# A four-layer model step on one core: zero products at the start, and new orders of work in the odd layer

## The chip, the cores and the metric

The kernel runs on one core of a Trainium2 chip. The metric is device time in microseconds, the median of the runs; the kernel before took 1620.36 us (three runs, 1618.04 to 1621.01). A core has TensorE (in the profile PE, with its weight loads as PEld), VectorE (DVE), ScalarE (ACT), GpSimd (POOL) and SyncE (SP), which run their own programs and meet at semaphores; SP issues all transfers here.

## The reference

All data are float32, x is 256 tokens by 1024. Two blocks follow each other:

- The first block has two layers. Each projects the RMS-normed x to 4096 columns, runs four retention heads and four attention heads of width 128 over the 256 tokens, gates them with silu, projects back (`w_out`) and adds; then it adds `sigmoid(rms_norm(x) @ w_ple_gate) * rms_norm(p @ w_ple)`.
- The second block has an even layer (an RWKV-7 recurrence beside a multiscale pool), an expert stage, an odd layer and a second expert stage. The odd layer is what the change touches:

```python
u = h @ w_in
q, k, v, u_s5 = jnp.split(u, ...)
q = apply_rope(rms_norm_2(q, q_norm), cos, sin)
k = apply_rope(rms_norm_2(k, k_norm), cos, sin)
o = diff_attention(q, k, v, lam)          # per head: softmax of map 0 minus lam times softmax of map 1, times v
o = rms_norm_2(o, subln, SUBLN_EPS) * (1.0 - lam_init)
o_ssm = s5_mixer(u_s5, ...)               # 32 state-space groups, gelu, then z * sigmoid(z @ w_glu)
return jnp.concatenate([o_attn, o_ssm], axis=-1) @ w_out
```

- An expert stage routes each token to 2 of 32 experts (hidden width 512) and reads the weights of all 32.

## The kernel before, in words

**Memory.** Projection weights come through a ring of six slots of 2 MB (`weight_ring`), in the order of `ring_chunks`. `g.send(sp, n)` (line 247) issues all chunks up to number n, each behind the semaphore that frees its slot; `g.chunk(pe, i)` makes TensorE wait for a chunk. The expert stages use the same slots and some areas of `arena`, `mix` and `hT` for their 2 MB pieces (`in_moe_weights`), six for a pair of experts; a loop over the pairs (line 2503 on SP, issuing through line 2490) loads a piece when the pair three before has released its place.

**The start (`first_layers`).** SP issues x of token tile 0 and x of tile 1, the resident constants (identity and small tables), the gain column, two ring chunks, and then the rest. For each tile ACT squares x in two halves with a sum (line 352) and takes a root (363); DVE inverts it and scales x into `x_normed` (368, 369). TensorE transposes the eight 128x128 squares of a tile (379) into two banks, and DVE writes them out to `hT` with the gain (391). The projections of the first chunks are 16 products of 128x512 each (808): unit 0 works on tile 0, then come the transposes of tile 1, then units 1 to 3. DVE handles tile 0 whole, its evacuation among it, before `eps` of tile 1.

**The odd layer (`odd_layer`).** Eight projections `project(j)` go to TensorE: 0 and 1 give u of the S5 groups (line 2085), 2 to 5 give q and k of the two token tiles, 6 and 7 give v of the tiles (322). SP waits for their count `s_prj` before it loads pieces of the expert stage into slots. TensorE's order is:

- projections 0 to 2, the S5 inputs (2100, 256 small products), projections 3 to 5;
- the S5 outputs in four steps a, each 32 products of K (2115) and 64 of the states (2122); ACT takes a gelu of each step (1902);
- project(6); transposes of q and k in four groups (2134), each behind the gelu of the same number, whose bank it takes, and all behind `s_qk`, DVE's rotation of q and k (1982 to 1994);
- the products of the GLU in two halves (2153), with scores(0) and scores(1) between them (2143, 2144); project(7);
- the head loop: transposes of the attention map (2182), scores(h + 2) for h = 0 and 1, product with v (2189 to 2191) once ACT has copied the map (1919). Ahead of head 2 stands the first part of the first output product (`out_part(0)`, line 2168, 8 products);
- the rest of the output products, then the router and the expert stage.

DVE runs `masked(h)` (adds the causal mask, takes the maximum; 2004 to 2010) and `attention(h)` (2016 to 2024) in the order m0, m1, a0, a1, the product of z with the sigmoid (2041), m2, m3, a2, a3. ACT runs `exps(h)` (1893) between them, the sigmoids (1912) and `copy_out(7)` (1885): exps 0 and 1, the sigmoids, copy_out(7), the copies of heads 0 and 1, exps 2 and 3, the copies of heads 2 and 3. `scores(h)` writes two banks that `masked(h - 2)` has read; the buffers `pb` and `attn` are double, by h % 2. The orders are written out by hand, and each engine follows its own.

```python
            for h in range(HT):
                if h == 2:
                    pe.wait_ge(s_z, 2)
                    pe.wait_ge(s_mk, 3)
                    out_part(0, (4, 5, 6, 7))
                pe.wait_ge(s_at, h + 1)
```

Of the kernel before, what the change touches and what calls it, by code (L numbers as in the profile page):

```python
# [13 lines left out]
P = 128  # L14
S = 256
TT = S // P
# [245 lines left out]
def bank2(ps):  # L262
    return ps[:, :].rearrange("p (a t) -> p a t", a=2)
# [156 lines left out]
def first_layers(g):  # L420
# [47 lines left out]
    s_tok = [g.sem(f"first{l}_ple_in_landed") for l in range(DEPTH)]  # L468
    s_wide = [g.sem(f"first{l}_wide_gains_landed") for l in range(DEPTH)]
    s_m, s_t, s_r, s_rc = g.sem("table_masked"), g.sem("tables_spread"), g.sem("bias_rows"), g.sem("bias_rows_copied")  # L470
    s_w, s_b = g.sem("bias_rows_written"), g.sem("bias_landed")
    norm_sems = TileNorm.sems(g, "first_norm")
    n_in = [TileNorm(g, norm_sems, 2 * l, (128, 144, 192)[l], gcol[l], (2, 3)) for l in range(DEPTH + 1)]
    n_ple = [TileNorm(g, norm_sems, 2 * l + 1, 160 + 16 * l, None, (2, 3)) for l in range(DEPTH)]
# [17 lines left out]
    with nc.Block() as block:  # L492
        @block.sync
        def _(sp):
            for tt in range(TT):
                sp.dma_start(g.x[:, tt, :], A["x"][0, tt * P:(tt + 1) * P, :]).then_inc(s_x[tt], 16)
            sp.dma_start(g.res[:, :], A["c_res"]).then_inc(s_res, 16)
            sp.dma_start(gcol[0], A["norm_g"][0]).then_inc(s_gain[0], 16)
            g.send(sp, 2)
            sp.wait_ge(s_m, 1)  # L500
            sp.dma_start(table[0:BUCKETS, :], A["rel_bias"]).then_inc(s_tab, 16)
            sp.dma_start(consts, A["c_first"]).then_inc(s_c, 16)
            sp.dma_start(ptok, A["p"][0, 0].rearrange("(a p) n -> p a n", p=P)).then_inc(s_tok[0], 16)
            for l in range(DEPTH):
                for i, name in enumerate(("q_norm_g", "k_norm_g")):
                    sp.dma_start(qkg[l][:, i:i + 1], A[name][l].rearrange("(d o) -> d o", o=1)).then_inc(s_qkg[l], 16)
            g.send(sp, SLOTS)
            sp.dma_start(gcol[1], A["norm_g"][1]).then_inc(s_gain[1], 16)
            sp.dma_start(gcol[2], A["even_norm_g"]).then_inc(s_gain[2], 16)
            for h in range(4):  # L510
                sp.wait_ge(s_rc, h + 1)
                sp.dma_start(scratch[h], rows[:, h, :]).then_inc(s_w, 16)
            for l in range(DEPTH):
                sp.dma_start(rgain[l], A["ret_norm_g"][l].partition_broadcast(P)).then_inc(s_wide[l], 16)
                sp.dma_start(pgain[l], A["ple_norm_g"][l].partition_broadcast(P)).then_inc(s_wide[l], 16)
            sp.wait_ge(s_w, 64)
            for h in range(4):

                for tt in range(TT):
                    src = bass.AP(scratch.tensor, h * P * 511 + 255 - tt * P, [[510, P], [1, (tt + 1) * P]])  # L520
                    dst = bias[:, h * 384 + tt * P:h * 384 + tt * P + (tt + 1) * P]
                    sp.dma_start(dst, src).then_inc(s_b, 16)
            g.send(sp, SLOTS + 3)
            sp.wait_ge(*layer[0].pt2(1))
            sp.dma_start(ptok, A["p"][1, 0].rearrange("(a p) n -> p a n", p=P)).then_inc(s_tok[1], 16)
            g.send(sp, per * DEPTH + SLOTS)
# [124 lines left out]
        def _(dve):  # L651
# [42 lines left out]
            def gated(q, j):  # L694
# [2 lines left out]
                link(dve, TT_(e[part(j)], e[part(j)], sig[j % 2], ALU.mult))  # L697
                TT_(g.x[part(j)], g.x[part(j)], e[part(j)], ALU.add).then_inc(q.gu.sem, 1)

            dve.memset(table[:, :], NEG).then_inc(s_m, 1)  # L700
            for tt in range(TT):
                n_in[0].eps(dve, tt)
# [91 lines left out]
        def _(pe):  # L794
# [29 lines left out]
            def e_in(l, j):  # L824
                tt, ch = divmod(j, 2)
                project_natural(g, pe, per * l + 10, pT, ps[6 + ch], tt, slice(ch * HALF, (ch + 1) * HALF)).then_inc(layer[l].e.sem, 1)

            pe.wait_ge(s_res, 16)
            n_in[0].transposes(pe, 0)
            for l in range(DEPTH):  # L830
                q, n = layer[l], n_ple[l]
                was = layer[l - 1] if l else None
# [954 lines left out]
def odd_layer(g, c0):  # L1787
# [49 lines left out]
    with nc.Block() as block:  # L1837
# [35 lines left out]
        def _(act):  # L1873
# [36 lines left out]
            for q in range(2):  # L1910
                act.wait_ge(s_gl, q + 1)
                act.activation(sig[:, 2 * q:2 * q + 2, :], bank2(ps[GLU_BANK[q]]), ACT.Sigmoid).then_inc(s_sg, 1)
            copy_out(7)
            for h in range(HT):
                if h == 2:
                    exps(2)
                    exps(3)
                act.wait_ge(s_tr, h + 1)
                act.copy(attnT[h % 2], ps[4 + h % 2][:, 0:W3]).then_inc(s_trc, 1)
# [22 lines left out]
        def _(dve):  # L1942
# [87 lines left out]
                        ins.then_inc(s_at, 1)  # L2030
                g.dve_steps.wait(dve)

            for h in range(0, HT, 2):
                masked(h)
                masked(h + 1)
                attention(h)
                attention(h + 1)
                if h == 0:
                    for q in range(2):
                        dve.wait_ge(s_sg, q + 1)  # L2040
                        TT_(g.mixT[:, 4 + 2 * q:6 + 2 * q, :], zT[:, 2 * q:2 * q + 2, :], sig[:, 2 * q:2 * q + 2, :],
                            ALU.mult).then_inc(s_z, 1)

            dve.wait_ge(s_oe, TT)
            link(dve, TT_(osq, osb, osb, ALU.mult))
# [30 lines left out]
        def _(pe):  # L2076
# [32 lines left out]
            pe.wait_ge(s_x, 2)  # L2109
            pe.wait_ge(s_bur, 1)  # L2110
            for a in range(HT):
                for d in range(STEP):
                    for i in range(4):
                        w = slice(32 * i, 32 * i + 32)
                        pe.matmul(ps[a][w, d * NK:S], v.K[w, a, d, :],  # L2115
                                  uT[w, a, 0:STEP - d, :].rearrange("p j k -> p (j k)"), start=(d == 0), stop=False,
                                  tile_position=(32 * i, 32 * i))
                for d in range(STEP):
                    for r in range(2):
                        for i in range(4):  # L2120
                            q = 4 * i + a
                            ins = pe.matmul(ps[a][32 * i:32 * i + 32, d * NK + 1:(d + 1) * NK], v.C[d + 1][:, r, q, :],  # L2122
                                            states((x_re, x_im)[r])[:, q, 0:NK - 1], start=False,
                                            stop=(d == STEP - 1 and r == 1), tile_position=(0, 32 * i))
                ins.then_inc(s_y, 1)
            pe.wait_ge(s_ev, 3)
            project(6)
            pe.wait_ge(s_qk, 4)
            for b in range(4):
                pe.wait_ge(s_ge, b + 1)  # L2130
# [17 lines left out]
            for q in range(2):  # L2148
                pe.wait_ge(s_ev, (4, 6)[q])
                for i in range(2):  # L2150
                    n = (2 * q + i) * P
                    for k in range(HT):
                        ins = pe.matmul(ps[GLU_BANK[q]][:, i * S:(i + 1) * S], w_glu[:, k, n:n + P], zT[:, k, :],  # L2153
                                        start=(k == 0), stop=(k == HT - 1))
                ins.then_inc(s_gl, 1)
                if q == 0:
                    pe.wait_ge(s_qT, 4)
                    scores(0)
                    scores(1)
            pe.wait_ge(s_ev, 5)  # L2160
            project(7)

# [10 lines left out]
            for h in range(HT):  # L2173
# [7 lines left out]
                for j in range(3):  # L2181
                    ins = pe.transpose(ps[4 + h % 2][:, j * P:(j + 1) * P], attn[h % 2][:, j * P:(j + 1) * P], ident)
                ins.then_inc(s_tr, 1)
                if h + 2 < HT:
                    scores(h + 2)
                pe.wait_ge(s_trc, h + 1)
                hs = slice(h * P, (h + 1) * P)
                w = attnT[h % 2]
# [675 lines left out]
```

## Time and profile before

| what | value |
|---|---|
| median of three runs | 1620.36 us |
| the profiled execution | 1619.47 us |
| its span (first to last instruction) | 1617.7 us |
| TensorE busy with products | 1355.6 us (84%), 9414 of them |
| DVE, ACT, POOL busy | 24%, 17%, 6% |
| mean granted clock of TensorE | 0.946 of full |
| data read from memory | 494 MB |
| transfers over the span | 307 GB/s in the mean, 428 to 429 GB/s in the expert stages |

The profile is one execution. The times of its rows start at the span's start; the 1.8 us between span and execution lie around it. A row of the timeline gives start, duration, engine and line of the kernel, operation, what is written from what, the number of instructions that it merges, and in brackets how long the engine was idle before and which event ended that. Products on TensorE overlap, so their durations are read from the distance of starts. "issue" in brackets means that the profile shows nothing that was waited for.

### The profile page before, as it was taken

Reading aid. Unit: us, or ns where it says so; the run is one execution under the profiler, and the core shown is the slowest. Engines: PE = TensorE matmul, PEld = TensorE weight load, DVE = VectorE, ACT = ScalarE, POOL = GpSimd, SP = SyncE. Lnnn points to the kernel's source line nnn. Section 1 sums busy time; section 2 is a strip of 40 time slices with the busy share of each in tenths; the row PEclk is TensorE's granted clock in tenths of the full one; section 3 lists DMA queues with packets and bytes.
Section 4 is the critical chain, followed back from the end, with each engine's and each line's share of the span. In section 5 each row is a group of like instructions: output and inputs, shape, how many; then the busy total and the mean of one; then the engine's idle time right before and its main releaser. Section 6 shows DMA issues by size and latency. Waiting matters only on the chain. (4 is left out here: it accounts for less than half of the span.)

```text
span 1617.7 us, 22089 instructions
## 1 busy us (share of the span) xinstructions
PE 1355.6 (84%) x9414; PEld 724.8 (45%) x9414; DVE 385.6 (24%) x787; ACT 278.3 (17%) x545; POOL 95.9 (6%) x98
## 2 busy tenths in 40 slices
PE   7999999999999999677677676899998767767676
PEld 3755457545879664232232323655553223232232
DVE  2331333313376531011010000266421001000011
ACT  1132310313223121210000000114211101111010
POOL 0000000000000007294000000000000000000000
PEclk9999999999999999898988999999999898899889
DMA  9822453234521199999999999933689999999997
GB/s 384 275 103 104 156 187 125 78 130 177 205 105 56 57 428 408 429 428 428 429 428 429 429 428 427 392 137 144 265 344 420 428 428 428 428 429 429 428 429 328
DMA packets 42092, 497.05 MB, mean 307 GB/s; under 512 B 6448, under 2 KB 9264, under 8 KB 11568
## 3 DMA queue, kind: packets, MB, share of 16 engines
q1 hardware_dynamic: 42032, 496.17, 74.5%
q8 instruction: 47, 0.77, 0.2%
q14 instruction: 13, 0.11, 0.0%
HBM read 494.06 MB, written 2.10 MB: 307 GB/s over the span
## 5 line engine op out<-in xcount | busy, mean ns | idle before, releaser
L2656 PE MATMUL banks<-weight_ring,arena 128*32 128x512 f32 x1920 | 289.2, 735 | 176.8 <-DMA weight_ring<-in_moe_weights 176.7
L2656 PEld LDWEIGHTS banks<-weight_ring,arena 128*32 128x32 f32 x1920 | 60.1, 122 | 386.6 <-DMA weight_ring<-in_moe_weights 197.0
L2579 DVE TENSOR_TENSOR arena<-arena,banks 64x512 f32<-64x512 f32 x32 | 22.1, 690 | 691.4 <-ACT arena L2527 691.4
L808 PE MATMUL banks<-weight_ring,hT 128*128 128x512 f32 x384 | 169.7, 599 | 1.5 <-DMA weight_ring<-in_ring_weights 1.5
L2667 PE MATMUL banks<-weight_ring,arena 128*32 128x512 f32 x1016 | 122.5, 610 | 29.7 <-DMA weight_ring<-in_moe_weights 15.0
L2638 PE MATMUL banks<-arena,x_normed 128*128 128x64 f32 x1024 | 119.9, 276 | 0.0
L2638 PEld LDWEIGHTS banks<-arena,x_normed 128*128 128x128 f32 x1024 | 119.7, 196 | 0.0
L808 PEld LDWEIGHTS banks<-weight_ring,hT 128*128 128x128 f32 x384 | 72.9, 192 | 88.1 <-issue 86.0
L322 PE MATMUL banks<-weight_ring,hT 128*128 128x512 f32 x256 | 112.3, 593 | 0.0
L2527 ACT ACTIVATE arena<-banks 64x512 f32<-64x512 f32 x32 | 18.9, 590 | 518.2 <-PE banks L2656 518.2
L2697 PE MATMUL banks<-arena 64*128 64x512 f32 x240 | 59.6, 615 | 21.0 <-ACT arena L2533 21.0
L2667 PEld LDWEIGHTS banks<-weight_ring,arena 128*32 128x32 f32 x1016 | 33.5, 111 | 93.3 <-issue 44.8
L322 PEld LDWEIGHTS banks<-weight_ring,hT 128*128 128x128 f32 x256 | 48.1, 190 | 57.2 <-issue 56.9
L322 PE MATMUL banks<-weight_ring,mix 128*128 128x512 f32 x128 | 55.9, 592 | 0.0
L804 PE MATMUL banks<-hT,weight_ring 128*128 128x256 f32 x256 | 55.9, 379 | 0.0
L804 PEld LDWEIGHTS banks<-hT,weight_ring 128*128 128x128 f32 x256 | 48.3, 190 | 6.4
L1389 PE MATMUL banks<-hT,weight_ring 128*128 128x256 f32 x224 | 49.0, 380 | 1.1 <-PEq L224 1.1
L2697 PEld LDWEIGHTS banks<-arena 64*128 64x128 f32 x240 | 20.6, 186 | 62.4 <-ACT arena L2533 48.2
L1389 PEld LDWEIGHTS banks<-hT,weight_ring 128*128 128x128 f32 x224 | 42.4, 190 | 7.7 <-issue 2.1
L2568 DVE TENSOR_TENSOR arena<-banks,arena 128x256 f32<-128x256 f32 x68 | 28.7, 424 | 71.8 <-PE banks L2638 71.7
L2533 ACT COPY arena<-banks 128x512 f32<-128x512 f32 x32 | 18.7, 585 | 144.9 <-PE banks L2667 144.9
L1721 POOL MEMSET arena<- 128x512 f32 x1 | 0.5, 524 | 614.9 <-PE banks L2656 614.9
(489 smaller groups left out, 1378.4 us busy)
## 6 DMA issues: line engine op xcount, KB each, us to landing
weight_ring<-in_moe_weights SPq DMA_DIRECT2D x183, 2048.0 KB, 25.8
weight_ring<-in_ring_weights SPq DMA_DIRECT2D x36, 2048.0 KB, 8.2
arena<-in_moe_weights SPq DMA_DIRECT2D x4, 2048.0 KB, 10.7
weight_ring<-in_ring_weights SPq DMA_DIRECT2D x4, 1024.0 KB, 4.9
mix<-in_moe_weights SPq DMA_DIRECT2D x2, 2048.0 KB, 16.1
arena<-in_moe_weights SPq DMA_DIRECT2D x3, 1024.0 KB, 12.6
hT<-in_moe_weights SPq DMA_DIRECT2D x2, 1024.0 KB, 9.7
arena<-in_c_even SPq DMA_DIRECT2D x1, 1440.0 KB, 6.4
```

What stands on the lines that cost most here:

```text
L322: ins = pe.matmul(bank, lhsT[:, k, tt * P:(tt + 1) * P], w[:, k, n], start=(k == 0), stop=(k == k_all - 1))
L804: ins = pe.matmul(bank[:, hh * S:(hh + 1) * S], w[:, k, h * P:(h + 1) * P], g.hT[:, k, :], start=(k == 0), stop=(k == KT - 1))
L808: ins = pe.matmul(bank, g.hT[:, k, half * P:(half + 1) * P], w[:, k, :], start=(k == 0), stop=(k == KT - 1))
L1389: ins = pe.matmul(bank[:, i * S:(i + 1) * S], w[:, kt, n:n + P], g.hT[:, kt, :], start=(kt == 0), stop=(kt == KT - 1))
L2527: act.activation(sil[0:2 * CAP, :], b_gu[0:2 * CAP, :], ACT.Silu).then_inc(s_sl, 1)
L2533: act.copy(y, b_dn[:, :]).then_inc(s_yc, 1)
L2568: dve.tensor_tensor(xg[:, k, :], (b_x, b_dn)[h][:, 0:256].rearrange("p (k j) -> p k j", k=4), gcol[:, k].unsqueeze(2).to_broadcast([P, 4, ...
L2579: dve.tensor_tensor(hid[0:2 * CAP, :], sil[0:2 * CAP, :], b_gu[2 * CAP:4 * CAP, :], ALU.mult).then_inc(s_h, 1)
L2638: ins = pe.matmul((b_x, b_dn)[k // 4][:, k % 4 * 2 * CAP:(k % 4 + 1) * 2 * CAP], g.xs[:, tt, k * P:(k + 1) * P], Pm[:, tt].rearrange("p e ...
L2656: ins = pe.matmul(b_gu[q:q + CAP, :], xg[:, 2 * quarter + k, e * CAP:(e + 1) * CAP], up_w(where, quarter, e)[:, which, k, :], start=(quart ...
L2667: ins = pe.matmul(b_dn[q:q + CAP, :], hidT[:, 2 * half + f, e * CAP:(e + 1) * CAP], down_w(at_pair[group], 4 + half, e)[:, f, nh * 512:(nh ...
L2697: pe.matmul(ps[2 * tt + nh][:, :], PT[r, tt * P:(tt + 1) * P], y[r, :], start=opens, stop=True, skip_group_check=True).then_inc(s_sum[2 * ...
```

## The change

It has two places. At the start, DVE first writes zeros to a 128x128 piece of `sT[0]`; TensorE waits for them, multiplies them 26 times into bank 7, goes on to the transposes of tile 0, and multiplies them four times more behind these. SP issues x of tile 1 behind the first ring chunk instead of ahead of the constants. In the odd layer, TensorE runs project(6) between the S5 steps 1 and 2, and scores(2) and scores(3) ahead of project(7) instead of in the head loop; DVE runs masked(2) ahead of the product with the sigmoid and masked(3) behind it; ACT runs exps(2) ahead of copy_out(7). Nothing else changes, and no value is computed differently.

```diff
@@ -468,7 +468,7 @@
     s_tok = [g.sem(f"first{l}_ple_in_landed") for l in range(DEPTH)]
     s_wide = [g.sem(f"first{l}_wide_gains_landed") for l in range(DEPTH)]
     s_m, s_t, s_r, s_rc = g.sem("table_masked"), g.sem("tables_spread"), g.sem("bias_rows"), g.sem("bias_rows_copied")
-    s_w, s_b = g.sem("bias_rows_written"), g.sem("bias_landed")
+    s_w, s_b, s_zero = g.sem("bias_rows_written"), g.sem("bias_landed"), g.sem("zeros")
     norm_sems = TileNorm.sems(g, "first_norm")
     n_in = [TileNorm(g, norm_sems, 2 * l, (128, 144, 192)[l], gcol[l], (2, 3)) for l in range(DEPTH + 1)]
     n_ple = [TileNorm(g, norm_sems, 2 * l + 1, 160 + 16 * l, None, (2, 3)) for l in range(DEPTH)]
@@ -492,10 +492,11 @@
     with nc.Block() as block:
         @block.sync
         def _(sp):
-            for tt in range(TT):
-                sp.dma_start(g.x[:, tt, :], A["x"][0, tt * P:(tt + 1) * P, :]).then_inc(s_x[tt], 16)
+            sp.dma_start(g.x[:, 0, :], A["x"][0, 0:P, :]).then_inc(s_x[0], 16)
             sp.dma_start(g.res[:, :], A["c_res"]).then_inc(s_res, 16)
             sp.dma_start(gcol[0], A["norm_g"][0]).then_inc(s_gain[0], 16)
+            g.send(sp, 1)
+            sp.dma_start(g.x[:, 1, :], A["x"][0, P:S, :]).then_inc(s_x[1], 16)
             g.send(sp, 2)
             sp.wait_ge(s_m, 1)
             sp.dma_start(table[0:BUCKETS, :], A["rel_bias"]).then_inc(s_tab, 16)
@@ -697,6 +698,7 @@
                 link(dve, TT_(e[part(j)], e[part(j)], sig[j % 2], ALU.mult))
                 TT_(g.x[part(j)], g.x[part(j)], e[part(j)], ALU.add).then_inc(q.gu.sem, 1)
 
+            dve.memset(sT[0][:, 0:P], 0.0).then_inc(s_zero, 1)
             dve.memset(table[:, :], NEG).then_inc(s_m, 1)
             for tt in range(TT):
                 n_in[0].eps(dve, tt)
@@ -825,8 +827,15 @@
                 tt, ch = divmod(j, 2)
                 project_natural(g, pe, per * l + 10, pT, ps[6 + ch], tt, slice(ch * HALF, (ch + 1) * HALF)).then_inc(layer[l].e.sem, 1)
 
+            def keep_clock(n):
+                for _ in range(n):
+                    pe.matmul(ps[7][:, 0:P], sT[0][:, 0:P], sT[0][:, 0:P], start=True, stop=True)
+
+            pe.wait_ge(s_zero, 1)
+            keep_clock(26)
             pe.wait_ge(s_res, 16)
             n_in[0].transposes(pe, 0)
+            keep_clock(4)
             for l in range(DEPTH):
                 q, n = layer[l], n_ple[l]
                 was = layer[l - 1] if l else None
@@ -1910,10 +1919,10 @@
             for q in range(2):
                 act.wait_ge(s_gl, q + 1)
                 act.activation(sig[:, 2 * q:2 * q + 2, :], bank2(ps[GLU_BANK[q]]), ACT.Sigmoid).then_inc(s_sg, 1)
+            exps(2)
             copy_out(7)
             for h in range(HT):
                 if h == 2:
-                    exps(2)
                     exps(3)
                 act.wait_ge(s_tr, h + 1)
                 act.copy(attnT[h % 2], ps[4 + h % 2][:, 0:W3]).then_inc(s_trc, 1)
@@ -2030,16 +2039,18 @@
                         ins.then_inc(s_at, 1)
                 g.dve_steps.wait(dve)
 
-            for h in range(0, HT, 2):
-                masked(h)
-                masked(h + 1)
-                attention(h)
-                attention(h + 1)
-                if h == 0:
-                    for q in range(2):
-                        dve.wait_ge(s_sg, q + 1)
-                        TT_(g.mixT[:, 4 + 2 * q:6 + 2 * q, :], zT[:, 2 * q:2 * q + 2, :], sig[:, 2 * q:2 * q + 2, :],
-                            ALU.mult).then_inc(s_z, 1)
+            masked(0)
+            masked(1)
+            attention(0)
+            attention(1)
+            masked(2)
+            for q in range(2):
+                dve.wait_ge(s_sg, q + 1)
+                TT_(g.mixT[:, 4 + 2 * q:6 + 2 * q, :], zT[:, 2 * q:2 * q + 2, :], sig[:, 2 * q:2 * q + 2, :],
+                    ALU.mult).then_inc(s_z, 1)
+            masked(3)
+            attention(2)
+            attention(3)
 
             dve.wait_ge(s_oe, TT)
             link(dve, TT_(osq, osb, osb, ALU.mult))
@@ -2109,6 +2120,9 @@
             pe.wait_ge(s_x, 2)
             pe.wait_ge(s_bur, 1)
             for a in range(HT):
+                if a == 2:
+                    pe.wait_ge(s_ev, 3)
+                    project(6)
                 for d in range(STEP):
                     for i in range(4):
                         w = slice(32 * i, 32 * i + 32)
@@ -2123,8 +2137,6 @@
                                             states((x_re, x_im)[r])[:, q, 0:NK - 1], start=False,
                                             stop=(d == STEP - 1 and r == 1), tile_position=(0, 32 * i))
                 ins.then_inc(s_y, 1)
-            pe.wait_ge(s_ev, 3)
-            project(6)
             pe.wait_ge(s_qk, 4)
             for b in range(4):
                 pe.wait_ge(s_ge, b + 1)
@@ -2157,6 +2169,8 @@
                     pe.wait_ge(s_qT, 4)
                     scores(0)
                     scores(1)
+            scores(2)
+            scores(3)
             pe.wait_ge(s_ev, 5)
             project(7)
 
@@ -2181,8 +2195,6 @@
                 for j in range(3):
                     ins = pe.transpose(ps[4 + h % 2][:, j * P:(j + 1) * P], attn[h % 2][:, j * P:(j + 1) * P], ident)
                 ins.then_inc(s_tr, 1)
-                if h + 2 < HT:
-                    scores(h + 2)
                 pe.wait_ge(s_trc, h + 1)
                 hs = slice(h * P, (h + 1) * P)
                 w = attnT[h % 2]
```

## Rows read from the trace of the kernel before

**Rows 1.** the chain that ended last, odd layer and second expert stage: start us, us, what

```profile
1111.68 0.43 PE banks L2143 x4
...
1198.41 7.00 PE banks L2656 x64
...
1216.69 7.05 PE banks L2656 x64
...
1364.83 0.04 SPq L2490
...
1394.21 0.04 SPq L2490
```

**Rows 2.** timeline of TensorE, start: start us, us, engine line op, [idle before]

```profile
8.39 1.94 PE L379 MATMUL banks<-resident_constants,x_normed 128*128 128x128 f32 x8 [8.39 <-DVE x_normed L369]
11.82 9.29 PE L808 MATMUL banks<-weight_ring,hT 128*128 128x512 f32 x16 [1.49 <-DMA weight_ring<-in_ring_weights]
20.94 1.04 PE L379 MATMUL banks<-resident_constants,x_normed 128*128 128x128 f32 x8
21.82 20.77 PE L808 MATMUL banks<-weight_ring,hT 128*128 128x512 f32 x48
```

**Rows 3.** timeline of ACT and DVE, start

```profile
4.25 0.63 ACT L352 ACTIVATE x_normed<-x 128x512 f32<-128x512 f32 x1 [2.24 <-DMA x<-in_x]
...
7.49 0.75 DVE L369 TENSOR_SCALAR x_normed<-x,small 128x1024 f32<-128x1024 f32 x1
...
9.59 1.47 DVE L391 TENSOR_TENSOR hT<-banks,arena 128x512 f32<-128x512 f32 x2 [1.35 <-PE banks L379]
```

**Rows 4.** windows: busy PE, PEld, DVE, ACT, POOL; granted clock, DMA share, GB/s

```profile
11.00:16.20 5.20, 4.38 (x5) 1.85 (x6) 1.03 (x4) 0.29 (x1) 0.00 (x0) 1.00 0.98 417
...
644.00:651.00 7.00, 3.84 (x24) 1.10 (x24) 0.00 (x0) 0.46 (x1) 5.52 (x3) 1.00 1.01 428
651.00:654.50 3.50, 3.37 (x16) 0.59 (x16) 0.00 (x0) 0.00 (x0) 0.00 (x0) 0.51 1.01 431
```

**Rows 5.** timeline of TensorE, odd layer

```profile
1089.34 1.29 PE L2115 MATMUL banks<-mix,arena 32*32 32x256 f32 x32
...
1091.58 1.29 PE L2115 MATMUL banks<-mix,arena 32*32 32x256 f32 x32
...
1095.27 0.86 PE L2122 MATMUL banks<-arena 128*32 128x63 f32 x45 [1.96 <-issue]
...
1097.28 0.96 PE L2122 MATMUL banks<-arena 128*32 128x63 f32 x51
1099.00 0.42 PE L2122 MATMUL banks<-arena 128*32 128x63 f32 x13 [0.77 <-issue]
...
1106.32 1.91 PE L2134 MATMUL banks<-resident_constants,x_normed 128*128 128x128 f32 x16
...
1124.49 0.55 PE L2182 MATMUL banks<-resident_constants,arena 128*128 128x128 f32 x3 [0.68 <-ACT arena L1885]
...
1133.86 0.49 PE L2189 MATMUL banks<-arena 128*128 128x128 f32 x2 [0.57 <-ACT arena L1919]
...
1135.69 0.49 PE L2189 MATMUL banks<-arena 128*128 128x128 f32 x2 [0.57 <-ACT arena L1919]
```

**Rows 6.** queues of the transfers, 1084 to 1102 us: packets, MB, share

```profile
q8 instruction: 3, 0.05, 1.5%
```

**Rows 7.** tile weight_ring, 0 to 12 us: loads of the ring, time to landing

```profile
L247 SPq DMA_DIRECT2D weight_ring<-in_ring_weights x5: 432/452/6370, 2.6 to 10.5; - x5
...
DMA to landing us min/median/max: 9.1/19.0/25.4
```

**Rows 8.** timeline of DVE, odd layer

```profile
1103.19 0.68 DVE L1994 TENSOR_TENSOR x_normed<-arena 128x512 f32<-128x512 f32 x1
...
1117.07 0.17 DVE L2010 TENSOR_SCALAR small<-small 128x4 f32<-128x4 f32 x1
```

**Rows 9.** timeline of ACT, odd layer

```profile
1120.44 1.09 ACT L1912 ACTIVATE mix<-banks 128x512 f32<-128x512 f32 x2
```

## The prediction

> **What bounds the kernel now.** I read the chain that ended last first. In the second expert stage one pass over a pair of experts takes 29.4 us, the distance of two issues of line 2490 [rows 1], while the same pass in the stage's beginning, with its weights already there, takes TensorE 18.3 us [rows 1]. So the passes wait for weights, and a quicker engine there buys nothing. What starts the stream is TensorE: slots of the ring come free when projections end. A gain ahead of an expert stage therefore moves the stream's start and lasts to the end; I count it in full. The rest of the reading is two stretches that TensorE sets: the first 21 us, and the odd layer (1038 to 1178 us).
>
> In the first stretch [rows 2] the reader should see three things. TensorE does nothing before 8.39 us, since x of tile 0 is scaled only from 7.49 on [rows 3]. Then come eight transposes, and the first projection at 11.82. Its sixteen products take 9.29 us where the next 48 need 20.77, or 0.43 each: 6.9 for sixteen. The 2.4 us between are TensorE at 1.2 GHz instead of 2.4: five products fill the 4.4 busy us to 16.2 [rows 4] (the granted clock there reads 1.00, so the level is read from the durations). The eight transposes take 1.94 us, and the same eight at 20.94 take 1.04.
>
> In the odd layer [rows 5] the S5 output steps run at 2.24 us each (1089.34 to 1091.58) until TensorE stops for 1.96 us before 1095.27 and for 0.77 before 1099.00, with nothing that it waits for. In this stretch the queue of instructions moved three packets [rows 6]. The second stop ends 3.73 us after the first, with 45 + 32 + 51 = 128 products between: I read both stops as the fetch of the next block of instructions, the first one behind weights.
>
> **The change, part by part: the start.** The edits are one step: zeros written by DVE, 26 products of them, four more behind the transposes, and x of tile 1 issued behind the first ring chunk.
> - *The 26 products.* No row shows a 128x128 product before 8 us; the nearest are the transposes, 0.24 us slow and 0.13 fast [rows 2]. DVE begins at 0.80, and a 128x128 write by it is 0.2 to 0.3 us, so they run from 1.1 to between 4.5 and 7.4. x scaled is ready for TensorE at 8.39: they cost nothing, with 1.0 us in hand at the slow end. If that cover is gone, each us of lateness costs one.
> - *What they buy.* The clock rose after 4.4 us of projection [rows 4]; 3.4 to 6.3 us of zeros should raise it once. But between their end and 8.39 TensorE is idle 1 to 3.9 us, and then has only eight transposes. In the expert stage the clock was 1.00 in a stretch with 3.84 us of work in 7 and an idle end, and 0.51 in the 3.5 us behind it [rows 4]. So the clock can fall once more before the projection. Ends: nothing, or all of the 2.4 us. I take the middle, 1.1: one fall, and a rise early in the projection.
> - *The first chunk.* It was issued at 2.6 and landed 9.1 us later [rows 7], at 11.7, which is what the projection waited for. 0.5 MB fewer lie ahead of it, at the 428 GB/s of rows with DMA full 1.2 us [rows 4]: it lands at 10.5. hT was ready at 11.06 (9.59 + 1.47 [rows 3]); with fast transposes 0.5 earlier, 10.55. So the projection starts at 10.7 rather than 11.82: 1.1 us. If the transposes and the four products run slow, they end at 10.33 + 0.96 = 11.3, and 0.5 is left.
> - *x of tile 1.* Its chain is two squares with their reads (1.6 us), root, inverse and scale, some 3.1 us in all by the rows of tile 0 [rows 3]. Landed at 11.8 behind the chunk, it is ready at 14.9; it is wanted when the first projection ends, at 17.5 to 18.7. Hidden. On SP's queue the constants and gain 0 move forward by one issue; the second chunk and all behind it have the same bytes ahead. Only if x came behind both chunks (some 17 us) would TensorE wait, up to 2.6 us.
> Sum of the start: 1.1 + 1.1 = 2.2 us, ends 3.5 and -1.5.
>
> The Trainium skill, TensorE: Matmul & The Clock Gate, Part 4 (PE-mode transpose), says that transposes do not count as work that brings the full clock. By that rule the fall before the projection is nearly certain, and the sum of the start would be nearer 1.2 than 2.2; the trace has transposes at 1.2 GHz ahead of a slow projection, which agrees and does not decide it.
>
> **The odd layer.** Times are those of before.
> - *project(6) between S5 steps 1 and 2.* Steps 0 and 1 end at 1091.6, project(6) at 1098.5 (a projection is 7.03 less overlap, 6.88), steps 2 and 3 without stops at 1103.0. While project(6) runs, the instruction block has 6.9 us to come. 208 further products at speed hold one more block end; its fetch now meets idle DMA, as the second stop did: 0.7 us, ends 0 and 2. So S5 ends at 1103.7. The transposes of q and k also wait for DVE, which rotates until 1103.87 [rows 8]: they begin at 1104.0 instead of 1106.32. ACT has the last gelu to 1104.4, which only the fourth group waits for. Gain here 2.35. Ends: 3 and 0.3. SP's load of a second-pair chunk waits for the end of S5 and moves from 1099.5 to 1103.7; DMA is idle there.
> - *scores(2), scores(3) ahead of project(7).* They wait for the masks of heads 0 and 1; the second ended at 1117.24 [rows 8], now 1114.9, and the second half of the GLU's products ends at 1114.4. So scores(2) has not to wait and scores(3) begins at 1115.3: 1.7 us for both (0.43 for each half of a head [rows 1]), 0 to 0.3 of waiting. project(7) ends at 1123.1 (before 1123.85, start of the head loop 1124.49 [rows 5]): the head loop begins at 1123.7.
> - *DVE.* masked(2) now needs no head loop: it ends about 1120.9, the two gate products (sigmoids ended 1121.5 [rows 9], now 1119.1) at 1122.2, masked(3) at 1124.4. exps(2) runs 1120.9 to 1122.8 behind its table load, and copy_out(7), queued behind it on ACT, is wanted at 1123.1: 0.3 us in hand. If mask 2 were a microsecond later, the head loop would start 0.7 later.
> - *The head loop.* Without scores between them, transposes and product of a head expose the copy, 0.57 us for each of two heads, as heads 2 and 3 did; a head takes 1.83 [rows 5]. Heads 0 and 1: 1123.7 to 1127.5 (before 1128.65). out_part(0) 3.43: to 1131.0. attention(2) is long done, exps(3) ends at 1128.5, attention(3) at 1130.3. So the 0.49 wait for DVE goes; heads 2 and 3 end at 1134.9 against 1136.6.
> Sum: 1.8 us, ends 3.7 and -0.7. The next limits are the copies of ACT. SP sends chunk (1,0) 4 us earlier, in idle DMA time; (0,4) still waits for the third output product, so the stream starts 1.8 us earlier.
>
> **The sum.** 2.2 + 1.8 = 4.0 us. The profiled execution took 1619.5 (span 1617.7); less 4.0, 1615.5. The median is 0.9 above it: 1616.4. A measurement can tell 0.2%, 3.2 us, from no change.
>
> **Rivals.**
> 1. *The zeros buy nothing*: the clock falls before the projection and rises as late as before. For: the idle time named, and rows 4. Against: at least one fall has to come and a rise not. Left: 1.1 + 1.8 = 2.9, or 1617.5. Chance 0.2.
> 2. *The clock holds*: 1.1 + 2.4 + 1.8 = 5.3, or 1615.1. Against: 1 to 3.9 idle us. Chance 0.12.
> 3. *The odd layer gives nothing*: the stops are not hidden but move behind project(6), 2.7 us; S5 ends at 1105.7 and the transposes begin 0.6 us earlier, which the exposed copies and scores(3) use up. For: nothing in the profile names the stops' cause. Against: three instruction packets, and 128 products between. Left 2.2, 1618.2. Chance 0.15. The Trainium skill, Runtime: NRT & Kernel Launch, § Instruction fetch mechanics, calls the cost of crossing a block mostly hidden; the trace differs if my reading holds (1.96 and 0.77 us).
> 4. *x of tile 1 comes behind both chunks*: TensorE waits 2.6 us, which leaves 0 + 1.8, 1619. Chance 0.05.
> 5. *Slower*: the 30 new products move every block end of TensorE's program. A pass holds some 142 products, a block 128, so it lies in two blocks or in three. If in three and only two are kept, each pass fetches again. A fetch beside weights took 5.2 us (about 1090.1 to 1095.27), and a pass has 29.4 - 18.3 = 11 us in hand: two fetches hide, three cost 4.6 us in each of some 13 passes, 60 us, 1680. It decides from 11 us a pass. Against: it needs the loop to end within 14 products of a block's end and more than two fetches. Chance 0.03. The same skill page says that a jump outside of two pages forces a fetch; no row shows one.
> The forecast itself has 0.45, with its own range 1615 to 1618.
>
> **How the numbers follow.** Faster by more than 0.2% (under 1617.1): four fifths of the forecast's case, 0.36; the clock holding, 0.12; under half of rival 1, 0.08; together 0.56. Slower: rival 5 and a fall of the clock at a worse place in the first expert passes, which TensorE sets, 0.06. The rest, 0.38, is no change. The range goes from 1614.0 (the clock holds, and the stops all go) to 1619.6 (rivals 3 and 4 in).
>
> **What would show it.** Right: line 808 first at 10.7 with sixteen products in 7 to 8.2 us; transposes of line 379 in 1.04; no stop of 1.96 us in S5, the transposes of q and k waiting for DVE at 1104 less the start's gain; head loop with four waits of 0.57 for ACT. Wrong: a first projection at 11.5 or later, or in 9 us; S5 stops of 2 us behind project(6); the head loop waiting for copy_out(7); waits for instructions in the expert loop.

## The result, and the profile after

The changed kernel took 1625.19 us (median of 20 runs, 1620.99 to 1629.13) where the kernel before took 1618.94 (20 runs on the same chip, 1617.1 to 1622.57). The ratio is 1.0036, interval 1.0029 to 1.0043: slower by 0.36%, where 0.24% faster was predicted. The profiled execution of after took 1622.34 us (span 1620.6), near the low end of its runs; where that matters it is said below. One count has to be known for the rows: a float32 product as written is two records of TensorE in a trace, each with a record of its weight load, and a transpose is one.

**The start.** TensorE's timeline of after (start us, us, engine line op, [idle before]):

```profile
1.05 7.70 PE L832 MATMUL banks<-arena 128*128 128x128 f32 x52 [1.05 <-DVE arena L701]
8.62 1.06 PE L379 MATMUL banks<-resident_constants,x_normed 128*128 128x128 f32 x8
9.52 1.06 PE L832 MATMUL banks<-arena 128*128 128x128 f32 x8
11.60 7.10 PE L810 MATMUL banks<-weight_ring,hT 128*128 128x512 f32 x16 [1.02 <-DMA weight_ring<-in_ring_weights]
18.54 1.04 PE L379 MATMUL banks<-resident_constants,x_normed 128*128 128x128 f32 x8
```

Against [rows 2] the start does what it was made for. The 26 products are 52 records here and run until 8.6 us; x of tile 0 is scaled at 8.47, so they just cover the wait for it. (In the traces of the five later runs that keep these products they last 7.95 to 8.66 us, and the transposes begin 0.4 to 1.2 us after x is scaled instead of 0.15; the wait for the first chunk covers that.) The clock stays up through these (1.06 us for eight, not 1.94) and through the projection (7.10 us, not 9.29). Tile 1 is transposed at 18.54 instead of 20.94: 2.4 us gained.

**The even layer.** The gain is whole at 465.38 us, where TensorE begins a run of 192 records of small products, 2.39 us earlier than before. The same stretch in TensorE's timeline, before and then after:

```profile
467.77 3.03 PE L1444 MATMUL banks<-arena 64*64 64x64 f32 x192
470.73 14.00 PE L322 MATMUL banks<-weight_ring,hT 128*128 128x512 f32 x32
```

```profile
465.38 3.03 PE L1453 MATMUL banks<-arena 64*64 64x64 f32 x192
471.85 15.59 PE L322 MATMUL banks<-weight_ring,hT 128*128 128x512 f32 x32 [3.44 <-issue]
```

This is a stop of 3.44 us that the kernel before does not have. It is marked "issue", so TensorE waited for nothing that the profile shows. The projections behind it take 1.59 us more. The windows of after say why (us, busy PE, PEld, DVE, ACT, POOL; granted clock, DMA share, GB/s):

```profile
466.00:468.00 2.00, 2.00 (x152) 2.00 (x145) 1.42 (x4) 0.00 (x0) 0.00 (x0) 1.00 0.87 369
468.00:470.00 2.00, 0.40 (x28) 0.45 (x21) 1.97 (x3) 0.00 (x0) 0.00 (x0) 1.00 0.98 418
470.00:472.00 2.00, 0.15 (x1) 0.15 (x1) 1.97 (x5) 0.00 (x0) 0.00 (x0) 1.00 0.29 115
472.00:474.00 2.00, 2.00 (x3) 0.71 (x3) 1.13 (x2) 0.00 (x0) 0.00 (x0) 0.53 0.03 8
```

After 3.4 us with TensorE idle the granted clock is 0.53, so it runs at 1.2 GHz: three products in 2 us. Stop and clock turn 2.4 us of lead into 2.7 of lag. And the DMA is at 0.98 for the first part of the stop, until 470 us. The queues of after, from 462 us to the end of the small products at 468.4, then from there to 473 (packets, MB, share):

```profile
q1 hardware_dynamic: 74, 1.21, 54.8%
...
weight_ring<-in_moe_weights SPq DMA_DIRECT2D x1, 2048.0 KB, 8.8
...
q1 hardware_dynamic: 70, 0.88, 45.8%
q8 instruction: 1, 0.02, 1.2%
```

There is one 2 MB load of expert weights, issued at 463.8. The one packet of instructions in these 11 us comes only after the products have run out, at about 469.45. I call the instructions that such a packet brings a block. By [rows 5] it is 128 records of products with their 128 weight loads (45 + 32 + 51 between the two stops of before), so 64 written products; the small ones use that up in 2.0 us.

**The odd layer.** TensorE's timeline of after:

```profile
1092.61 0.97 PE L2136 MATMUL banks<-arena 128*32 128x63 f32 x55
1096.47 0.33 PE L2136 MATMUL banks<-arena 128*32 128x63 f32 x9 [2.90 <-issue]
1096.73 8.82 PE L322 MATMUL banks<-weight_ring,hT 128*128 128x512 f32 x16
...
1109.96 1.97 PE L2146 MATMUL banks<-resident_constants,x_normed 128*128 128x128 f32 x16
...
1122.19 7.13 PE L322 MATMUL banks<-weight_ring,hT 128*128 128x512 f32 x16
1130.00 0.55 PE L2196 MATMUL banks<-resident_constants,arena 128*128 128x128 f32 x3 [0.68 <-ACT arena L1894]
1131.11 0.49 PE L2201 MATMUL banks<-arena 128*128 128x128 f32 x2 [0.57 <-ACT arena L1928]
```

The new orders are there (scores ahead of project(7), four waits of 0.57 in the head loop), but the two stops of before, 1.96 and 0.77 us [rows 5], have become one of 2.90, ahead of project(6) and followed by 1.7 us of slow clock in it. Its place fits a count: before's first stop stands 32 + 19 = 51 records behind the end of S5 step 1, this one 9 records ahead of that end. It has moved by 60 records, which is what 30 written products are. Counted from the layer's first product (1038.15 before, 1040.20 after), the transposes of q and k begin at 69.76 instead of 68.17, and the routing behind the layer at 136.65 instead of 134.34: 2.3 us lost where 1.8 were to be won.

**The sum.** The routing behind the even layer begins 3.6 us late (587.61 against 583.99): the 2.7, and 0.9 of another fall of the clock (0.94 over 560 to 588, 1.00 before). With the odd layer's 2.3 that is 5.9 us; the medians differ by 6.3. The profiled execution itself shows only 2.9, since its two expert stages ran 3.0 us quicker than before's; the medians show no such gain.

### The profile page after: what moved, and what is told of

Same layout as the page of the kernel before. It is cut to its first block and busy times, and to the rows that moved or that the text cites. A ratio compares the mean times of both kernels' runs of the same rounds, so it can differ in the third digit from the quotient of the medians.

```text
span 1620.6 us, 22210 instructions
## 1 busy us (share of the span) xinstructions
PE 1357.0 (84%) x9474; PEld 732.5 (45%) x9474; DVE 383.8 (24%) x788; ACT 278.1 (17%) x545; POOL 96.1 (6%) x98
## 5 line engine op out<-in xcount | busy, mean ns | idle before, releaser
L2668 PE MATMUL banks<-weight_ring,arena 128*32 128x512 f32 x1920 | 285.4, 726 | 183.7 <-DMA weight_ring<-in_moe_weights 183.3
L2679 PE MATMUL banks<-weight_ring,arena 128*32 128x512 f32 x1016 | 119.0, 595 | 28.4 <-issue 14.7
```

The lines of the kernel that those rows point to most:

```text
L2668: ins = pe.matmul(b_gu[q:q + CAP, :], xg[:, 2 * quarter + k, e * CAP:(e + 1) * CAP], up_w(where, quarter, e)[:, which, k, :], start=(quart ...
L2679: ins = pe.matmul(b_dn[q:q + CAP, :], hidT[:, 2 * half + f, e * CAP:(e + 1) * CAP], down_w(at_pair[group], 4 + half, e)[:, f, nh * 512:(nh ...
```

## The experiments

There are two questions. Which half of the change costs? And what makes the stops? The expectations name three theories:

- Theory A: it matters *where in TensorE's program the blocks of instructions end*. The 30 added products move every end by about half a block, so that one falls at the end of the small products.
- Theory B: the new orders of the odd layer cost by themselves.
- Theory C: the late x of tile 1, or the clock that the large zero products raise, costs further on.

A fourth was not written down before the runs: it matters *when the work runs*, and whatever comes 2.4 us earlier meets the weights' load (theory D).

| kernel | median us | ratio to before | even stop | odd stops | layers, us |
|---|---|---|---|---|---|
| after | 1625.19 | 1.0036 (1.0029 to 1.0043) | 3.44 | 2.90 | +5.9 |
| start alone | 1623.6 | 1.0028 (1.0018 to 1.0038) | 3.99 | 3.63 | +5.3 |
| odd layer alone | 1616.48 | 0.9987 (0.9978 to 0.9997) | none | none | -1.9 |
| before + 30 small | 1627.47 | 1.0047 (1.0033 to 1.0061) | 3.83 | 3.62 | +9.9 |
| before + 64 small | 1619.66 | 1.0012 (1.0003 to 1.0021) | none | 1.82 | +1.5 |
| after + 34 at start | 1615.15 | 0.9981 (0.9969 to 0.9992) | none | none | -1.2 |
| after + 34 later | 1615.22 | 0.998 (0.9971 to 0.9989) | none | none | -1.9 |
| after, loads held | 1615.42 | 0.9977 (0.9968 to 0.9986) | 0.98 | 0.20 | -2.3 |
| both of these | 1614.59 | 0.9977 (0.9968 to 0.9986) | none | none | -2.9 |

"Layers" is worked out from each trace: how much later than before the even layer's routing begins, plus how much longer the odd layer takes to its own. Added to the median before (1618.6 to 1618.9) it gives the medians to within 1.2 us, but for the two with 34 added (2.3 and 1.5): what happens in the layers passes through both expert stages. The even and odd stops are those marked "issue" in each layer's part of TensorE's timeline, one trace for each kernel. All added products are of zeros or constants, into a bank whose contents nothing reads then.

### The start alone

```diff
-            for tt in range(TT):
-                sp.dma_start(g.x[:, tt, :], ...)
+            sp.dma_start(g.x[:, 0, :], A["x"][0, 0:P, :]).then_inc(s_x[0], 16)
...
+            g.send(sp, 1)
+            sp.dma_start(g.x[:, 1, :], A["x"][0, P:S, :]).then_inc(s_x[1], 16)
...
+            keep_clock(26)
             n_in[0].transposes(pe, 0)
+            keep_clock(4)
```

> The start change alone (26 + 4 zero products, x of tile 1 later), the odd layer as before. Theory A (block ends): TensorE's program arrives in blocks of 64 written products, a fetch of one waits behind a 2 MB load of weights, and 30 new products move every block end; so the start gains 2.4 us up to the projection at 12 us, the even layer loses some 5 us (a stop of 3.4 us before line 322 behind the 96 small products at 465 us, and products at half clock behind it), and the odd layer's stops change too: 1622 to 1625 us. Theory B (the odd layer's new order is what costs): 1616 to 1618 us and no stop at 470 us.

Slower by 0.28%, with both stops and the order of S5 as before. Tile 1 is transposed at 18.56, as in after. So the loss belongs to this half, which rules theory B out, and it does not come from the first 20 us themselves.

### The odd layer alone

```diff
             for a in range(HT):
+                if a == 2:
+                    pe.wait_ge(s_ev, 3)
+                    project(6)
...
+            scores(2)
+            scores(3)
             pe.wait_ge(s_ev, 5)
             project(7)
```

> The new orders of the odd layer alone, the start as before. Theory A: block ends lie where they lay before, so no stop at 470 us; in the S5 outputs the block end that brought the 1.96 us stop now falls behind project(6), and the odd layer is 1.5 to 2.5 us faster: 1616 to 1618 us. Theory B (the order costs by itself, since project(6) waits or scores are exposed): 1621 us or more, with the transposes of q and k at least 1 us later than before.

Faster by 0.13%. The layer reaches its routing at 132.66 after its first product instead of 134.34: 1.68 us, and the q and k transposes come 2.40 earlier (predicted: 1.8 and 2.35). Here both of before's stops are gone: project(6), 7 us of only 16 records, runs from 1089.75, and a packet of instructions moves while it does (between 1091.25 and 1091.5).

### Thirty small products in front of before

```diff
...
+            pe.wait_ge(s_zero, 1)
+            for _ in range(30):
+                pe.matmul(ps[7][0:32, 0:32], sT[0][0:32, 0:32], sT[0][0:32, 0:32], start=True, stop=True, tile_position=(0, 0))
             pe.wait_ge(s_res, 16)
```

> The kernel before with 30 products of 32x32 by 32 columns of zeros in TensorE's idle time ahead of 8 us: no work is wanted there, the loads stay in their order, only block ends move by 30 products. Theory A: the start gains nothing (within 1 us), and the stop of about 3.4 us at 470 us appears: 1622 to 1625 us. Theory C (it is the late x of tile 1, or the clock raised by large zero products, that costs later): no stop at 470 us, and 1618 to 1620 us.

This is the deciding one: 30 products of 32x32 that run while TensorE would be idle, and nothing else (DVE writes their zeros first, as in after). TensorE's timeline:

```profile
1.05 3.41 PE L831 MATMUL banks<-arena 32*32 32x32 f32 x60 [1.05 <-DVE arena L700]
8.67 1.94 PE L379 MATMUL banks<-resident_constants,x_normed 128*128 128x128 f32 x8 [4.22 <-DVE x_normed L369]
...
11.99 9.00 PE L809 MATMUL banks<-weight_ring,hT 128*128 128x512 f32 x16 [1.38 <-DMA weight_ring<-in_ring_weights]
...
474.51 15.75 PE L322 MATMUL banks<-weight_ring,hT 128*128 128x512 f32 x30 [3.83 <-issue]
...
1102.14 0.47 PE L2126 MATMUL banks<-arena 128*32 128x63 f32 x9 [3.62 <-issue]
```

The start is that of before to 0.3 us, slow clock and all, and the small products of the even layer begin at 467.65 instead of 467.77. So nothing runs 2.4 us earlier, x of tile 1 comes as before and no large product raises the clock: theories C and D have no stop here. Both stops are there, at the same places in the program (behind the 192 records, and 9 records ahead of the end of S5 step 1), and the kernel is 0.47% slower. Theories C and D are out. The clock falls inside the stop, too: 0.74 over 472 to 474.5, without one product in it.

### Sixty-four in all: after with 34 more, and before with 64

```diff
             n_in[0].transposes(pe, 0)
             keep_clock(4)
+            for _ in range(34):
+                pe.matmul(ps[7][0:32, 0:32], sT[0][0:32, 0:32], sT[0][0:32, 0:32], start=True, stop=True, tile_position=(0, 0))
```

> The kernel after with 34 further products of 32x32 by 32 columns behind the four zero products: 64 in all, a whole block, so block ends lie again where they lay before. They take 1 to 2 us, of which the idle 1 us ahead of the first projection hides most. Theory A: no stop at 470 us, no stop of 2.9 us in the S5 outputs, 1615 to 1618 us. Theories B and C: as the kernel after, 1622 us or more.

64 written products are 128 records and their 128 loads, one whole block. After with 34 more small ones behind the four is 0.19% faster than before instead of 0.36% slower. Its timeline:

```profile
11.22 2.33 PE L840 MATMUL banks<-arena 32*32 32x32 f32 x68
13.48 7.13 PE L810 MATMUL banks<-weight_ring,hT 128*128 128x512 f32 x16
20.45 1.04 PE L379 MATMUL banks<-resident_constants,x_normed 128*128 128x128 f32 x8
...
1096.62 1.29 PE L2131 MATMUL banks<-mix,arena 32*32 32x256 f32 x32
```

The 34 delay the first projection to 13.48 and eat nearly all of the start's gain, yet 10 us come back against after, and its trace has no stop in either layer.

The same number in front of before, to see what one whole block does by itself (the edit of the section above, with 64 for 30):

> The kernel before with 64 products of 32x32 by 32 columns ahead of 8.4 us, a whole block of 256 instructions (e3_pad30 has 30). They take about 7.3 us of the idle 7.3. Theory A: no stop at 470 us, stops in the S5 outputs as in the kernel before (1.96 and 0.77 us): 1618 to 1620 us. If added products cost by their number, not by where block ends fall, it is slower than e3_pad30's 1627.5 us.

More than twice the added products cost 0.12%, not 0.47%. There is no even stop, and S5 stops for 1.82 at the place of [rows 5]:

```profile
12.88 9.42 PE L809 MATMUL banks<-weight_ring,hT 128*128 128x512 f32 x16 [2.45 <-DMA weight_ring<-in_ring_weights]
...
471.93 14.00 PE L322 MATMUL banks<-weight_ring,hT 128*128 128x512 f32 x32
...
1095.18 0.86 PE L2126 MATMUL banks<-arena 128*32 128x63 f32 x45 [1.82 <-issue]
```

Most of what it loses is at the start: the first projection waits 1.1 us longer for its chunk. Why was not tried. The odd layer adds 0.4: behind the stop of 1.82 the clock falls (0.50 over 1097 to 1099 us), which it did not behind before's 1.96 (1.00 over 1095.2 to 1097), so that the next 96 records take 3.84 us instead of 2.2.

### The loads held back

```diff
             for j, n in enumerate((3, 5, 7, 9)):
                 sp.wait_ge(s_prj, n)
+                if j == 2:
+                    sp.wait_ge(s_A, 6)
                 weights(0, j, ring[j], first)
...
-            sp.wait_ge(s_prj, 6)
+            sp.wait_ge(s_y, 2)
             weights(0, 1, ring[1], first)
```

> The kernel after, block ends as there, but two 2 MB loads are issued later: the third of the first expert pair in the even layer only once 96 small products ahead of line 322 are done (some 3 us later), and the second piece in the odd layer only after S5 step 1 (some 5 us later). Theory A1 (the fetch of a block waits until the load issued ahead of it has run): the stop of 3.44 us at 470 us and that of 2.90 us in the S5 outputs shrink to 0 to 1 us, no products at half clock behind them, 1614 to 1617 us. Theory A2 (a block's fetch takes as long whatever the loads do; only the place of the block ends counts): the stops stay above 2 us, 1623 to 1627 us.

Theory A has two parts: where a block ends, and a load of weights that the fetch stands behind. The expectation calls it A1 if both are needed and A2 if the place alone counts. Here every block end stays where it is in after; only two loads of 2 MB leave later (the even one at 468.63 instead of 463.8, the odd one 53.9 us after its layer's first product instead of 49.0). TensorE's timeline, and the queues from 462 to 468.4 us, where after's fetch had not come:

```profile
469.45 13.89 PE L322 MATMUL banks<-weight_ring,hT 128*128 128x512 f32 x32 [0.98 <-issue]
...
1090.28 0.33 PE L2138 MATMUL banks<-arena 128*32 128x63 f32 x9 [0.20 <-issue]
1090.54 7.13 PE L322 MATMUL banks<-weight_ring,hT 128*128 128x512 f32 x16
...
1102.48 1.97 PE L2148 MATMUL banks<-resident_constants,x_normed 128*128 128x128 f32 x16 [0.34 <-DVE x_normed L2005]
```

```profile
q8 instruction: 1, 0.02, 1.1%
```

The packet now goes ahead of the load, the stops shrink from 3.44 to 0.98 and from 2.90 to 0.20, the clock holds through both (the projections take 13.89 and 7.13), and the kernel is 0.23% faster than before. Both parts of theory A are needed for the big stop.

How far they shrink can be read from the packet. Seen in narrow windows, it moves at 469.45 in after and at 466.90 here, 2.55 us earlier, and the even stop is 2.46 shorter. In the odd layer, counted from its first product, the packet moves at 53.85 and 51.09, 2.8 earlier, and the stop is 2.70 shorter. In all eleven stops of these traces TensorE goes on 2.3 to 2.6 us after such a packet began to move. The 0.98 that is left fits this: by the count the block before ended after 64 of the 192 records, at about 466.5, and the products went on 3.0 us later, while the 128 records of a block of these small products last 2.0. In after the same count gives 5.5 us. So a fetch with nothing in its way is, by this estimate, already too slow for the small products, and the load adds the rest. This is a reading of the rows; no run tried it. The transposes of q and k now wait for DVE, as forecast.

### The 34 at another place, and both cures

```diff
             pe.wait_ge(*layer[DEPTH - 1].ec(8))
-            for _ in range(22):
+            for _ in range(46):
+                pe.matmul(ps[7][0:32, 0:32], ident[0:32, 0:32], ident[0:32, 0:32], start=True, stop=True, tile_position=(0, 0))
+            for _ in range(10):
                 pe.matmul(ps[7][:, 0:P], ident, ident, start=True, stop=True)
```

> The kernel after with 34 more products at the end of the first layers: 46 of 32x32 by 32 columns and 10 large ones stand where 22 large ones stood, in time that waits for the last scaled x. Block ends behind that place lie where they lay in the kernel before. Theory A: no stop at 470 us nor in the S5 outputs, and without the 1.9 us by which e4_pad64's products delayed the first projection: 1612.5 to 1615 us. If the ten large products are too few to hold the clock, the transposes behind them take twice as long and up to 2 us of this are lost.

At the end of the first layers TensorE multiplies constants anyway while it waits; 46 small and 10 large in place of 22 large add the same 34 without touching the start. The stops are gone again. But against what I had expected the kernel is not faster than the one with the 34 at the start. Windows of this kernel and, behind it, of the one with both edits:

```profile
399.00:402.00 3.00, 3.00 (x91) 2.87 (x91) 1.38 (x2) 1.21 (x3) 0.00 (x0) 1.00 0.65 147
402.00:406.30 4.30, 4.30 (x30) 4.26 (x27) 0.92 (x2) 1.69 (x4) 0.00 (x0) 0.60 0.91 385
```

```profile
399.00:402.00 3.00, 3.00 (x93) 2.96 (x90) 1.38 (x2) 1.37 (x4) 0.00 (x0) 1.00 0.74 213
402.00:404.40 2.40, 2.32 (x20) 2.13 (x20) 0.89 (x2) 1.43 (x2) 0.00 (x0) 1.00 1.02 437
```

Behind 92 records of 32x32 the clock fell to 1.2 GHz in one profile and held in the other; where it fell, the next transposes started 1.6 us later (406.12 against 404.49). A fall of this kind comes in some of the traces at other places too: the 40 records of constants ahead of the odd layer's routing take 4.71 us at a clock of 1.00 in this kernel and in the odd layer alone, and 5.9 to 6.2 in the other three mended ones (0.78 with the loads held), whose odd layers gain 0.9 us instead of 1.7.

> e6_pad_late and e5_hold together. Theory A1: the two mend the same stops, so together they give what the better one gives, 1612.5 to 1615 us. If holding loads costs something further on (a piece that lands late at 590 or 1190 us), it shows here as up to 3 us above e6_pad_late.

Both edits together gave the lowest median, 1614.59 (1612.26 to 1615.81), 0.23% under before and 10.6 us under after. Its ratio's interval is that of the loads held back alone, so which of the four mended versions is best is not settled; that each beats both kernels is.

## Why the prediction was wrong

**The step that failed** is the sum, which carries no term for what the 30 new products do to the rest of TensorE's program. The thought stands in rival 5: "the 30 new products move every block end of TensorE's program". I looked for its harm only in the expert loop, where a jump could fetch again, and gave it 0.03. Its premise happened; its place and price did not: no pass of the loop stops for "issue" longer than 0.5 us, as before, and the harm, 5.1 us in the even layer and 4.1 against plan in the odd one, fell in straight-line code. The odd layer's reading held the general rule already: stops of 1.96 and 0.77 [rows 5] came where many small products meet a block end beside a load. What was missing is the question where *else* such a stretch is, once the ends move. The even layer has it: 192 records in 3.03 us, with a 2 MB load issued 1.6 us ahead of them, in the kernel before as well (466.19 and 467.77).

**The unit of counting** failed beside it. A float32 product as written is two products in the records, each with a weight load. I took the 26 for 26 records: hence 3.4 to 6.3 us for them (7.70 measured) and an idle gap before the transposes that does not exist. The block of 128 and the pass of 142 products are records too, and I set the 30 written products beside them. They are 60 records, 0.47 of a block, which displaces every end nearly as far as it can be.

**The start**, point by point. Gain at tile 1: 2.2 forecast, 2.4 measured, by other terms. The clock gave all of its 2.2 (9.29 to 7.10), so rival 2, with 0.12, is what happened there. The projection started at 11.60, not 10.7: 0.2 of the 1.1. It still waited for its chunk, which was issued 0.48 earlier and took 9.3 us to land instead of 9.1; moving 0.5 MB behind a load did not bring it forward by the 1.2 us of that many bytes. x of tile 1 was scaled from 14.67 to 15.42 and hidden, as forecast. So the start's 2.2 came out by luck in its parts: the clock gave twice its 1.1, and the earlier chunk a fifth of its own.

The Trainium skill, TensorE: Matmul & The Clock Gate, Part 4 (PE-mode transpose), has transposes not count as work for the full clock, and from that the prediction took a fall before the projection as nearly certain. The trace shows no fall: products run to 8.6 us, then come the eight transposes and the four more products, to 10.6. TensorE was idle only in the 1.02 us behind them, so the rule was hardly put to the test.

**The odd layer** alone came out right: 1.68 for 1.8, transposes 2.40 for 2.35, the head loop's four waits of 0.57 as listed, and ahead of it the same 0.68 for copy_out(7) as before. Only the 0.7 us forecast for one more block end did not come: S5 had no stop, and DVE ended last at the transposes (0.74 of waiting). The reading that the block arrives while project(6) runs held with the ends where they were. In after the end moved to nine records *ahead* of project(6), which I had not checked; rival 3, by which the stops move and the layer gives nothing, was nearer, but it too kept the ends in place.

**The sum.** Predicted -4.0. In the layers: start -2.4, even stop and clock +5.1, a fall at 560 to 588 +0.9, odd layer +2.3, together +5.9; medians +6.3. That a stop of 3 us costs 1.6 to 1.7 more in clock was in none of my terms. The 0.9 is one fall in one profile; start alone and the 30 products have none at that place (4.71 us for the 40 records there, 6.24 in after).

**Left open.** After's profiled execution is 2.9 us under its own median; start alone and the 30 products had stops of 3.6 to 4.0 us, after's profile 3.44 and 2.90. How the stops vary from run to run was not measured. Why the two kernels with 34 more products gain 1.5 to 2.3 us more than their layers show is open too.

## What to carry to other kernels

Adding or removing instructions on an engine changes everything behind it: count the added instructions in the trace's units, as a share of a block, and look for each stretch where the engine uses up a block in 2 or 3 us (both places here) while a large load is in flight. If a change that should help hurts, add instructions up to a whole block as a test; if that restores it, the ends are the cause. Then either keep the padding or, sturdier, issue the load behind the small products, which cured it here without moving an end.

## What the runs showed of the hardware

- A packet of 16 KB of instructions came only when the products had run out while a 2 MB load was moving (stop 3.44 and 2.90 us; up to 3.99), and ahead of the load when this was issued later (0.98 and 0.20). TensorE went on 2.3 to 2.6 us after the packet began to move, in all eleven stops of these traces. The Trainium skill, Runtime: NRT & Kernel Launch, § Instruction fetch mechanics, calls the crossing of such a boundary mostly hidden. Most are, here too (48 packets of instructions in after, two such stops over 0.5 us); these are not, and 30 products of no effect cost 0.47%, the medians 8.8 us apart.
- Behind a stop of 2.9 to 4.0 us TensorE ran at half its clock for a time (0.50 and 0.53 over the 2 to 2.5 us behind the even stops of the 30 products and of after), and the work behind it took 1.3 to 2.7 us more. Behind a stop of 1.8 to 2.0 the clock fell in one kernel and held in the other; behind one of 0.98 it was 1.00.
- Products of zeros kept the clock up: with 52 records of 128x128 ahead of the transposes and 8 behind, transposes and projection ran at full speed; behind 60 and 128 records of 32x32 they ran slow (eight transposes in 1.94 us; the 60 had also ended 4.2 us before, the 128 only 0.4).
